# Two chunk scans of a RWKV-7 mixer: the inverse of one chunk beside the state part of the chunk before it

## What is computed

```python
def step(S, inp):
    r_t, w_t, k_t, v_t, kk_t, b_t = inp
    sa = -jnp.einsum("bhvk,bhk->bhv", S, kk_t)
    S = S * w_t[:, :, None, :] + sa[..., None] * b_t[:, :, None, :] + v_t[..., None] * k_t[:, :, None, :]
    return S, jnp.einsum("bhvk,bhk->bhv", S, r_t)

s_fwd_c, y_fwd_c = rwkv_scan(zero_state, fc, 0, reverse=False)
s_bwd_c, y_bwd_c = rwkv_scan(zero_state, fc, 1, reverse=True)
_, y_fwd_x = rwkv_scan(s_fwd_c, fx, 0, reverse=False)
_, y_bwd_x = rwkv_scan(s_bwd_c, fx, 1, reverse=True)
```

## Time and profile before

| | us |
|---|---|
| median of 3 runs (lowest, highest) | 2203.51 (2200.98, 2205.61) |
| span of the profiled execution, first to last instruction | 2192.6 |
| first scan, PE's first weight load to DVE's last state | 213.05 to 438.17 |
| second scan, the same | 1462.60 to 1679.71 |

### The profile page before, as it was taken

The page is one execution under the profiler, slowest core; times in us unless marked ns, Lnnn a source line. Parts: engine busy times, 40 slices in busy tenths (PEclk is TensorE's granted clock), DMA queues, the critical chain, the costliest instruction groups (busy, mean ns, idle before and its releaser), DMA issues. The chain is left out here.

```text
span 2192.6 us, 51555 instructions
## 1 busy us (share of the span) xinstructions
PE 1952.2 (89%) x22829; PEld 1569.6 (72%) x22829; DVE 1039.9 (47%) x1721; ACT 754.5 (34%) x1380; POOL 298.3 (14%) x381
## 2 busy tenths in 40 slices
PE   4985888898899999899998998968888899998988
PEld 1662878753578887688886766737876458998988
DVE  1536666572733333433332216476665363545544
ACT  1334333224632322332221114353332453435432
POOL 2103333202000111100001001043331120100000
PEclk7997999999999999999999998979999999999999
DMA  8513000020113333133236742000001114554543
GB/s 326 188 49 115 5 4 4 4 72 1 39 61 97 90 102 106 39 115 110 83 115 238 286 163 60 28 1 4 5 5 44 32 39 145 177 172 144 176 152 125
DMA packets 143452, 203.96 MB, mean 93 GB/s; under 512 B 6718, under 2 KB 123672, under 8 KB 137088
## 3 DMA queue, kind: packets, MB, share of 16 engines
q1 hardware_dynamic: 141728, 198.96, 27.1%
q0 software_dynamic: 1504, 1.71, 0.2%
HBM read 199.61 MB, written 1.05 MB: 92 GB/s over the span
## 5 line engine op out<-in xcount | busy, mean ns | idle before, releaser
L330 DVE TENSOR_TENSOR W_low<-RING,W_high 128x1024 fp32r<-128x1024 f32 x268 | 329.2, 1232 | 464.2 <-ACT W_high L327 463.9
L366 PE MATMUL BANK<-H_high,W_high 128*128 128x512 f32 (+2 forms) x1472 | 520.2, 353 | 19.2 <-ACT H_high L632 8.9
L368 PE MATMUL BANK<-H_high,W_low 128*128 128x512 f32 (+2 forms) x1472 | 515.5, 350 | 0.0
L367 PE MATMUL BANK<-H_low,W_high 128*128 128x512 f32 (+2 forms) x1472 | 515.4, 350 | 0.0
L327 ACT ACTIVATE W_high<-RING 128x1024 fp32r<-128x1024 f32 x268 | 281.1, 1052 | 598.2 <-PE BANK L368 576.8
L366 PEld LDWEIGHTS BANK<-H_high,W_high 128*128 128x128 f32 (+1 forms) x1472 | 280.5, 191 | 67.4 <-issue 26.4
L367 PEld LDWEIGHTS BANK<-H_low,W_high 128*128 128x128 f32 (+1 forms) x1472 | 280.8, 191 | 36.8 <-issue 0.9
L368 PEld LDWEIGHTS BANK<-H_high,W_low 128*128 128x128 f32 (+1 forms) x1472 | 280.2, 190 | 37.3
L1259 PE MATMUL BANK<-RING,WORK 64*64 64x64 f32 x4352 | 162.6, 222 | 13.8 <-issue 7.9
L1259 PEld LDWEIGHTS BANK<-RING,WORK 64*64 64x64 f32 x4352 | 144.7, 134 | 26.7 <-issue 9.8
L1259 PE MATMUL BANK<-RING 64*64 64x64 f32 (+1 forms) x3840 | 101.5, 255 | 43.9 <-DVE RING L1165 30.2
(11 more groups left out here) (307 smaller groups left out, 2824.9 us busy)
## 6 DMA issues: line engine op xcount, KB each, us to landing
RING<-w_in_dram SPq DMA_DIRECT2D x46, 1024.0 KB, 5.4
RING<-w_ffn_in_dram SPq DMA_DIRECT2D x44, 1024.0 KB, 5.2
lation_weights_ffn<-w_mod_dram SPq DMA_DIRECT2D x24, 1024.0 KB, 6.2
RING<-w_ffn_out_dram SPq DMA_DIRECT2D x20, 1024.0 KB, 5.1
tion_weights_opening<-w_mod_dram SPq DMA_DIRECT2D x8, 1024.0 KB, 8.5
ulation_weights_norm<-w_mod_dram SPq DMA_DIRECT2D x8, 1024.0 KB, 7.0
on_weights_features<-w_mod_dram SPq DMA_DIRECT2D x8, 1024.0 KB, 5.0
RING<-w_out_dram SPq DMA_DIRECT2D x8, 1024.0 KB, 5.2
```

Of the source, the lines that this page charges most:

```text
L330: low_ready.mark(nc.vector.tensor_tensor(self.part(1, c), self.raw(c), self.part(0, c).bitcast(FP32), ALU.subtract))
L366: nc.tensor.matmul(out, w[0], x[0], start=start, stop=False)
L367: nc.tensor.matmul(out, w[0], x[1], start=False, stop=False)
L368: return nc.tensor.matmul(out, w[1], x[0], start=False, stop=stop)
```

## The change

In step `i`, PE still makes the grams and the inverse of chunk `i`, and now also the state part of chunk `b = i - 1`, cut into ten groups of 16 or 8 matmuls that stand in the merges of chunk `i`: "between" the two products of a merge or "behind" the second. After the last step the state part of chunk 7 follows by itself, without the state's own update, which nobody reads. The matmuls are the same but for that one update: 3,712 in the first scan become 3,680, and 3,520 become 3,488.

`GRAM_X`, `BK_TOK` and `ARB` are double, the inverse has three parts of which a chunk uses two, `DEC` has four slots, `WS` is no longer `LM`, and the banks are divided otherwise. The decayed operands are no longer written to `QR` and `BK`: ACT writes the exponentials over `EXCL` and `INCL`, and DVE multiplies in place there and in `BB`; the copy `QR_KEPT` (L1171) goes. The subtractions of `exponents` and one half of the unit matrix's addition move from DVE to POOL. `Y` is no longer cleared: the first two chunks of a segment are put by ACT (`y_put`), the others added by DVE (`y_add`). Before and behind the scans no engine's list changes.

```diff
-    DEC = [sb(f"decay_{d}", [P, PAIRS]) for d in range(NDIR)]
+    DEC = [sb(f"decay_{d}", [P, 4, PAIRS]) for d in range(NDIR)]
...
+    EXCL = [carve(WORK, F0 + (5 + d) * WIDTH * 4, PAIRS, TOK) for d in range(NDIR)]
+    INCL = [carve(WORK, F0 + (7 + d) * WIDTH * 4, PAIRS, TOK) for d in range(NDIR)]
+    QUERIES = carve(WORK, F0 + 5 * WIDTH * 4, 2, NDIR, PAIRS, TOK)
...
+    K_DECAYED = [scratch(PAIRS, HD) for _ in range(NDIR)]
+    T_PARTS = [scratch(3, PAIRS, HD) for _ in range(NDIR)]
+    GRAM_X = [[scratch(PAIRS, 2, HD) for _ in range(2)] for _ in range(NDIR)]
...
+    BK_TOK = [[scratch(2, PAIRS, HD) for _ in range(2)] for _ in range(NDIR)]
+    ARB = [[scratch(PAIRS, HD) for _ in range(2)] for _ in range(NDIR)]
...
+    def inverse(d, i):
+        return T_PARTS[d][:, 0:2] if i % 2 == 0 else T_PARTS[d][:, 0:3:2]
...
+        B_LT = lambda d: 4 * d
+        B_L = lambda d: 4 * d + 1
+        B_TURN = lambda d: 4 * d + 2
+        B_STATE = lambda d: 4 * d + 3
...
+                def exponents(i):
+                    at = tokens_of(1, i)
+                    whole = INCL[1][:, :, at.stop - 1:at.stop].to_broadcast([P, PAIRS, CHUNK])
+                    pool.wait_ge(*at_step(s_exp, i, 2))
+                    nc.gpsimd.tensor_tensor(EXPO[:, 0], whole, EXCL[1][:, :, at], ALU.subtract)
+                    s_expo.mark(nc.gpsimd.tensor_tensor(EXPO[:, 1], whole, INCL[1][:, :, at], ALU.subtract))
...
-                    pool.wait_ge(*at_step(s_bk_tok[d], i))
+                    pool.wait_ge(*at_step(s_bk_turned[d], i))
...
+                    s_ops[d].mark(nc.gpsimd.tensor_tensor(K_DECAYED[d], KD[d][:, :, tokens_of(d, i)], GROWTH[d], ALU.mult))
...
+                exponents(0)
+                for d in range(NDIR):
+                    operands(0, d)
+                for i in range(STEPS):
...
+                            if l == 1:
+                                pool.wait_ge(*at_step(s_first[d], i, 1, 1))
+                                s_eye[d].mark(nc.gpsimd.tensor_tensor(inverse(d, i)[:, 1], inverse(d, i)[:, 1], lanes(eye_heads[:]), ALU.add))
+                        if i + 1 < STEPS:
+                            if l == 1:
+                                exponents(i + 1)
+                            if l >= 4:
+                                operands(i + 1, l - 4)
...
+                    if i >= 4:
+                        act.wait_ge(*at_step(s_st[d], i - 3))
...
+                    nc.scalar.activation(DEC[d][:, i % 4].unsqueeze(2), INCL[d][:, :, at.stop - 1:at.stop], ACT.Exp, scale=-KAPPA)
+                    s_grown.mark(nc.scalar.activation(GROWTH[d], incl, ACT.Exp, scale=KAPPA))
+                    nc.scalar.activation(EXCL[d][:, :, at], excl, ACT.Exp, scale=-KAPPA)
+                    act.wait_ge(*at_step(s_grown, i, 2, d + 1))
+                    s_exp.mark(nc.scalar.activation(INCL[d][:, :, at], incl, ACT.Exp, scale=-KAPPA))
...
+                for i in range(STEPS):
+                    b, more = i - 1, i + 1 < STEPS
+                    if more:
+                        exps(i + 1, 0)
...
+                        if more and l == 1:
+                            exps(i + 1, 1)
+                        for d in range(NDIR):
+                            if l == 2:
+                                bk_token_major(i, d)
+                            if b >= 0 and l == 3:
+                                w_out(b, d)
+                            if b >= 0 and l == 4:
+                                sa_out(b, d)
+                            if l == NL and has_y(b) and puts(b):
+                                y_put(b, d)
...
+                        v_token_major(i, d)
...
+                    nc.vector.tensor_tensor(BB[d][:, :, at], BB[d][:, :, at], GROWTH[d], ALU.mult)
+                    nc.vector.tensor_tensor(EXCL[d][:, :, at], KK[:, :, at], EXCL[d][:, :, at], ALU.mult)
+                    s_qr[d].mark(nc.vector.tensor_tensor(INCL[d][:, :, at], Z[:, Z_R:Z_R + PAIRS, at], INCL[d][:, :, at], ALU.mult))
...
+                def new_states(b):
...
+                        dve.wait_ge(*at_step(s_ds[d], b, 1, 1))
+                        s_add[d].mark(nc.vector.tensor_tensor(STATE[d], STATE[d], pairs(B_STATE(d), 0), ALU.add))
                     for d in range(NDIR):
...
+                        dve.wait_ge(*at_step(s_add[d], b, 1, 1))
+                        s_st[d].mark(nc.vector.tensor_tensor(STATE[d], STATE[d], DEC[d][:, b % 4].unsqueeze(2).to_broadcast([P, PAIRS, HD]), ALU.mult))
...
+                for i in range(STEPS):
+                    b, more = i - 1, i + 1 < STEPS
+                    gram_out(i, 0)
+                    for d in range(NDIR):
+                        first_level(i, d)
+                        arb_out(i, d)
+                    gram_out(i, 1)
+                    for l in range(1, LEVELS):
+                        if l == NL and has_y(b) and not puts(b):
+                            for d in range(NDIR):
+                                y_add(b, d)
+                        for d in range(NDIR):
+                            merge_level(i, l, d)
+                        if l == 1 and b >= 1:
+                            new_states(b - 1)
+                        if more and l in (2, 3):
+                            operands(i + 1, l - 2)
+                new_states(STEPS - 2)
+                for d in range(NDIR):
+                    y_add(STEPS - 1, d)
...
+                        pe.wait_ge(*at_step(s_v_tok[d], i))
+                        pe.wait_ge(*at_step(s_t[d], i, LEVELS))
...
+                    def first():
                         for d in range(NDIR):
...
+                            pe.wait_ge(*at_step(s_gram_out[d], i, 1, 1))
+                        s_turned_1.mark(side_by_side(HD, straight(0), across(1))[1])
+                    def second():
+                        pe.wait_ge(*at_step(s_turned_1, i, 1, 1))
+                        zero, one = side_by_side(HD, across(0), straight(1))
+                        s_bk_turned[0].mark(zero)
+                        s_bk_turned[1].mark(one)
+                    return first, second
...
+                def w_products(b):
...
+                    own = lambda d, first: (B_STATE(d), 0, CROSS, lambda j: EXCL[d][:, j, tokens_of(d, b)], lambda j: STATE[d][:, j], first, not first)
+                    other = lambda d, first: (B_STATE(d), 0, STAY_OTHER, lambda j: GRAM_X[d][b % 2][:, j, 0], lambda j: V_X[d][:, j], first, not first)
+                    def first():
                         for d in range(NDIR):
...
+                            pe.wait_ge(*at_step(s_gram_out[d], b, 1, 1))
+                            pe.wait_ge(*at_step(s_v_tok[d], b, 1, 1))
+                            pe.wait_ge(*at_step(s_st[d], b))
+                        s_w_1.mark(side_by_side(HD, own(0, True), other(1, True))[1])
+                    def second():
+                        pe.wait_ge(*at_step(s_w_1, b, 1, 1))
+                        one, zero = side_by_side(HD, own(1, False), other(0, False))
+                        s_w[1].mark(one)
+                        s_w[0].mark(zero)
+                    return first, second
...
+                def level(i, l, between, behind):
...
+                    if between:
+                        between()
...
+                        pe.wait_ge(*at_step(s_x1_out[d], i, NL, l))
+                        if l == 1:
+                            pe.wait_ge(*at_step(s_arb[d], i, 1, 1))
+                            pe.wait_ge(*at_step(s_eye[d], i, 1, 1))
...
+                    if behind:
+                        behind()
+                def with_v_turned(i, b):
...
+                        pe.wait_ge(*at_step(s_bk_tok[d], i, 1, 1))
+                        if has_y(b):
+                            turn, from_sa = side_by_side(HD, v_turned(i, d), y_from_sa(b, d))
+                            s_y[d].mark(from_sa)
+                        else:
+                            turn = side_by_side(HD, v_turned(i, d))[0]
+                        s_v_turned[d].mark(turn)
...
+                for i in range(STEPS):
+                    b = i - 1
+                    if b >= 0:
+                        w, y, ds = w_products(b), y_products(b), state_products(b)
+                    else:
+                        w = y = ds = (None, None)
+                    if not has_y(b):
+                        y = (None, None)
+                    turned = bk_turned(i)
+                    sa = ((lambda: sa_product(b, 0)), (lambda: sa_product(b, 1))) if b >= 0 else (None, None)
+                    y_and_v = lambda: with_v_turned(i, b)
+                    grams(i)
+                    level(i, 1, None, turned[0])
+                    level(i, 2, turned[1], w[0])
+                    level(i, 3, w[1], sa[0])
+                    level(i, 4, sa[1], y[0])
+                    if y[1]:
+                        y[1]()
+                    level(i, NL, y_and_v, ds[0])
+                    if ds[1]:
```

(72 more changed lines are left out.)

327 lines of the change are left out of this document (119 added, 208 removed).

## The result

The changed kernel takes 2211.54 us (median of 19 runs, 2200.15 to 2224.36), the kernel before in the same comparison 2200.98 us (19 runs, 2189.93 to 2209.12): ratio 1.0057, 95% interval 1.0040 to 1.0073. It is slower by 10.6 us in the medians, 12.5 us by the ratio, where 11.6 us less were forecast. Longer executions of the changed kernel are those with a lower mean granted clock (2200.15 us at 0.956, 2224.36 us at 0.942), and the profiled one, 2203.26 us with a span of 2201.5 us, is one of the short ones.

The account below looks back on a forecast made before the run. PE's instruction packets were taken to set the scans' pace: steps 414.0, ends 13.0, starts of scans 0.8 and of steps 2.8 sum to 430.6 us against 442.2, 11.6 us less, so 2192 us; range 2174 to 2206 us.

Parts of the forecast that it names:

- What bounds the kernel: In both scans, PE's program arrives in packets of 252 instructions, 3.83 us each, near balance with the data chain.
- the chain's 69.6 us: State part moved beside the merges in 14 steps: 10 x 5.3 + 4 x 4.15 us off the chain of data.
- rival A: In the scans, packets stay a side cost and the 69.6 us leave the path: about 2134 us, chance 0.05.
- What a packet costs then: In the scans' steps, 3.74 us a packet, between 3.60 and 3.83: (56.9 + 53.8) x 3.74 = 414.0 us.
- the starts of steps: POOL's mask of merge 2 comes later but mostly hides: 0.2 us a step allowed, 14 x 0.2 = 2.8 us.
- Rival B: In the scans, a packet stays at 3.83 us: sum 440.6 us, time 2202 us, no change to speak of, chance 0.17.
- The two ends: Behind each scan's last step the state part runs alone: 6.5 us twice, 13.0 us.
- rival C: At a step's start, seven POOL operations delay merge 2's mask: 21 us instead of 2.8, time 2210 us, chance 0.09.
- The start: Ahead of a scan's first product, one more exponential and one more wait on ACT: 0.4 us per scan, 0.8 us.
- The 10.9 us between span and median: Whole kernel: the runs' median lies 10.9 us above the profiled span, added to 2181.0 us to give 2192 us.

Follow-up runs that it names:

- after_cover: The changed kernel with BK's first turn between merge 1's two first products and DVE masking the second gram earlier: 2213.01 us, ratio 1.0059 to the kernel before.
- The cover with `y` ahead: The changed kernel with BK's first turn between merge 1's first products and the last chunk's `y` products ahead of `sa`: 2203.15 us, 1.0019 to the kernel before.

## Why the prediction was wrong

**What bounds the kernel** was read rightly, and so was "the packets set the pace in nearly every step, and the chain's 69.6 us mostly become longer waits for issue": packets of 252 instructions, 59 and 55 of them, issue waits doubled, hardly a gain from the data (one packet more costs 3.4 to 3.8 us; the placing is worth up to 55 us with half the instructions and 5 to 8 us with all). The Trainium skill's rule in "Runtime: NRT & Kernel Launch", "Instruction fetch mechanics", on which rival A stood, was rightly given little: the rule has the crossing mostly hidden, and here a packet more costs 3.4 to 3.8 us.

**The step that failed** is "What a packet costs then": "I take 3.74 us, midway between the quick steps' 3.64 and today's 3.83". The eight steps took 221.9 + 210.5 = 432.4 us for 110.7 packets, 3.91 us each, where the forecast had 416.8 with the starts of steps: 15.6 us too low. The 3.64 of the quick steps in the earlier trace rows was not a rate that shorter data waits would reach everywhere: the distance between the starts of two packets in the trace has a median of 3.79 us in both scans before, and 3.84 and 3.89 us after, and single distances scatter around it (before, eight in ten lie between some 3.5 and 4.5 us). The changed kernel has quick steps too, 26.95 us, and no more of them. The data waits of the kernel before lengthened the mean of 3.83 little; for the most part they lay inside it, as the undone placing shows. Rival B, a packet at 3.83 us and no change, was the nearest reading of the steps.

**The second term**, "The two ends", 6.5 us each, is near what they take at the full clock (6.42 us on PE, 6.89 with DVE's last addition of `y`, in the run with the long matmuls). On PE they took 9.8 and 9.4 us, nearly all at the 1.2 GHz level: with DVE's last addition, which ends at 450.05 and 1694.53 us, 10.3 + 9.9 = 20.2 us instead of 13.0. What PE did before its clock fell in the first scan, from its timeline and two windows:

```profile
435.82 0.47 PE L1292 MATMUL BANK<-RING,WORK 32*32 32x32 f32 x23 [1.99 <-issue]
```

```profile
432.00:437.30 5.30, 3.18 (x172) 2.77 (x172) 1.92 (x6) 0.45 (x2) 0.00 (x0) 1.00 0.01 3
437.30:439.80 2.50, 0.85 (x36) 0.69 (x32) 1.48 (x5) 0.66 (x2) 0.00 (x0) 0.50 0.04 7
439.80:449.60 9.80, 8.43 (x192) 7.33 (x192) 0.42 (x1) 1.42 (x4) 0.00 (x0) 0.50 0.02 3
```

It stood 1.99 us for issue in the last merge, and from 437.3 us on the clock was at the 1.2 GHz level to the end of the scan. The prediction used the clock in no term; the end in the earlier trace rows from which it took 6.44 us was itself partly at the lower level:

```profile
430.00:437.00 7.00, 6.48 (x208) 6.27 (x208) 1.37 (x5) 1.42 (x4) 0.00 (x0) 0.76 0.02 5
```

The runs with long matmuls show that it is the lack of work for PE in the last step that costs the clock; which of the stops there does it they don't tell. So slower instead of the same: rival B's 440.6 us and these 7.2 us are 447.8 us. By terms, 15.6 us in the steps, 7.2 us at the ends and 0.8 us less at the starts are the 22.0 us between the forecast of 430.6 and the measured 452.6.

**The rest**, 452.6 us measured against that 447.8, is some 5 us. Of these, 1.6 and 1.7 us are PE's waits for L1244 at the end of the two last steps. The prediction had no term for this: the last state update went, but the one before it, which the next chunk's grams used to cover, now stands between the last step and the part behind it. No run takes this wait away, so that it adds to the time is read from the trace alone; no stop for issue stands behind it. The remaining 1.5 us lie within the steps and stay open; each of the two traces is a single execution, and such differ by more than that. They aren't the wait for L1207 (after_cover) and hardly POOL's row: **rival C** has 1.2 and 1.0 us of waits for L1092, the masks' median is 731 ns, the mask of merge 2 starts 6.9 us after the second step's grams, as forecast, and the run that undoes its order is not clearly faster. **The start** of a scan cost nothing that can be seen: PE's waits ahead of the first products are 14.2 and 15.5 us, after 14.9 and 15.3.

The 10.9 us between span and median are not the time around the span: in the runs here an execution takes 1.8 us more than its span, and the rest is a short execution against the median. It was added on both sides, so the gain that was forecast doesn't hang on it.

Expectations failed as well. The pair in one pass differs by 11 us, not 40 to 70: the changed kernel with its placing undone is 44 us slower there than the kernel before, of which the start of a step explains some 27 us. The placing was worth 55 us in one pass, not 15 to 45. `y` ahead of `sa` gave 4 to 6 us, where 2 to 3 or under 1.5 were expected, and the kernel before with less work gained 10.9 us, not 7 to 9. The cover with `y` ahead came out 8 us faster, inside theory A's range, though the cover alone went by theory B; what the cover is worth beside the other edit stays open.

## What to carry to other kernels

Where an engine's waits without a semaphore come at a fixed number of instructions, that count times the mean distance of the packets acts as a floor: here an order that frees the chain of data gained nothing until instructions went. Test it by adding a packet of empty ones, then look for products that can be left out (0.5% here) or need fewer passes (5.5%, at lower precision). And look at what follows the last step of a pipelined loop: there PE was left without cover and lost its clock as well as its time, and an update that each step used to hide stood open.

## What the runs showed of the hardware

With one-pass products, and a third of the scan's time with PE idle, the granted clock was 0.50 to 0.52 through both scans, where it is 0.96 and 0.95 with fp32, and the scans were still 63 and 58 us shorter before the change. Eight long matmuls in the last step, 32 instructions, held the clock at 1.00 for the 6.4 us behind it, where it was 0.50 and 0.53 without them. A packet of matmuls with a single column, which PE runs through in little over 1 us, costs 3.4 to 3.8 us, nearly as much as one of full products.
